# Low parts of four heads and of all mixing inputs computed by the vector engine in PSUM, and stage entries re-ordered, in a hybrid two-block model on one core

## The chip, the cores and the metric

The kernel runs on one core of one Trainium2 chip. The metric is the device time of one execution in microseconds (us). Five engines work side by side: TensorE (PE, matrix products into PSUM), VectorE (DVE), ScalarE (ACT), GpSimd (POOL) and SyncE (SP, which issues the weight loads). They order their work by semaphores alone.

## What is computed

The reference chains two blocks over 16 meta tokens and 256 tokens of width 1024. Block one mixes two branches (a gated recurrence of 8 heads, "hg", and a latent attention, "mla"), projects the mixture, and ends with a feed-forward part. Block two runs two layers of a convolution beside a sparse attention. Cut to what the change touches:

```python
# block one
o = rms_norm(o, norm_g) * silu(g)                       # hg heads
y_a, y_b = o @ w_hg_o, mla @ w_mla_o
mixed = (gate_a * y_a + gate_b * y_b) @ w_out           # "mix"
h = h + rms_norm(mixed, mix_post_g)
gt, up = split(rms_norm(h, ffn_pre_g) @ w_ffn_in)
h = h + rms_norm((silu(gt) * up) @ w_ffn_out, ffn_post_g)
# block two, twice
y = concat([silu(layer_norm(conv)) * silu(zc), attention * silu(za)]) @ w_out_2[l]
h = layer_norm(ALPHA * h + y, post_ln_g, post_ln_b)
```

## The kernel before

Activations lie transposed: 128 features on the partitions, tokens along the free axis (256, or 272 with the meta tokens), so a width of 1024 is 8 tiles c = 0 to 7. Each weight product is made from three fast products: every operand x is rounded to a high part (x_hi) and a low part x_lo = x - x_hi, and `three` (L603) issues w_hi·x_hi, w_hi·x_lo and w_lo·x_hi. One `chunk` (128 output features) is 8 steps of three matmuls, 24 in all. `chunks_together` (L629) interleaves two or three chunks step by step, so that the first steps need only the first tiles of x; the last two steps (`tail`) run side by side at the end.

**Weights.** SP loads items of 256 columns into a ring of 3 slots. Each item is two pieces. ACT rounds a piece into w_hi (`round_piece`, L1264) after the chunk that frees one of the 4 buffers; POOL subtracts it into w_lo (`lo_piece`, L1139), and that frees the slot. POOL's program is one fixed list, in which the x subtractions (`lo_x`, L1153) stand between the weight subtractions.

**Entry of a stage.** PE can begin a stage when the first x_hi and x_lo are there, w_lo is there, and the PSUM bank (`bank_free`, L581) has been read. Where it would wait, the program puts in dummy products (`turns_over`, L686). The entries concerned are:

- **hgo**, eight chunks of the output product of the hg heads, in turns on PSUM banks 0 and 1. Its input y_hg is made by DVE (L1930), rounded by ACT (L1469), subtracted by POOL (L1196). DVE then multiplies each chunk in its bank by gate_a (L1944) and adds the gated mla part into `ya` in SBUF (L1945); that add frees the bank. Ahead of these, `gate_mla` (L1918) multiplies the eight mla chunks by gate_b, all operands in SBUF.
- **mix**, the projection. Its input is `ya`, rounded by ACT (L1474, each behind a weight piece) and subtracted by POOL (L1202).
- **ffi**, entered through `add_normed` (L1948: scale, then add to hT), **L0h**, the entry of block two through the same helper, **L1h** behind the first layer's normalisation (ACT writes hT and x_hi, L1691 and L1692).
- **wo**, the output product of a layer. Its eight inputs are four conv tiles (ACT Silu L1644, DVE product L2167) and four attention tiles (DVE L2173 out of PSUM), all rounded by ACT (L1610) and subtracted by POOL (L1238). The last chunk before it is za 3, whose 8 steps `z_chunks` (L208) spreads over the last attention steps; ACT reads it out at L1654 behind the Silu of three gates (L1649), and that frees the bank. x_hi is still read by za 3, so no new x_hi may be written before its end. PE turns the attention output by transposes (L1072) just ahead of wo.

Of the kernel before, what the change touches and what calls it, by code (L numbers as in the profile page):

```python
# [176 lines left out]
for _c in range(DC):  # L177
    PLN_DVE += [f"b{_c}"] + ([f"a{_c + 2}"] if _c + 2 < DC else [])
# [28 lines left out]

def z_chunks(l, s):  # L208
# [72 lines left out]
OUT, _outs = [], dict(chunk_out=0, gated=0, h_mid=0, h_ready=0, state=0)  # L281
GATED = ["L0a0", "L0a1", "L1a0", "L1a1"] + [f"hgo{_j}" for _j in range(4)] + [f"ffi{2 * _j + 1}" for _j in range(FFN_ITEMS)]
for _n, _m in ORDER:
    _by = "gated" if _n in GATED else "h_mid" if _n.startswith("mix") else "h_ready" if _n == "ffo" \
        else "state" if _n == "S" else "chunk_out"
# [9 lines left out]
def bass_blocks(nc, a, out):  # L295
    ctx = ExitStack()
    with ctx:
# [95 lines left out]
        ya, f_sq = z(DC, SEQ), z(DC, SEQ)  # L393
# [184 lines left out]
        def _(pe):  # L578
# [302 lines left out]
            chunks_together([part("hgo", c) for c in range(2)], (y_hi, y_lo), 0, x_ready("hg"))  # L881
            for c in range(2, DC):
                chunk(*part("hgo", c), (y_hi, y_lo))
            turns_over(3, 3)
            linear_norm("post", [lambda: chunks_together([part("mix", c) for c in range(2)], X, META, x_ready("mix"))]
# [17 lines left out]
            turns_over(3, BANK[CHUNK[part("ffi", 1)]])  # L903
# [33 lines left out]
            for l in range(DEPTH2):  # L937
# [5 lines left out]
                turns_over((12, 10)[l], BANK[CHUNK[part(f"{T}g", 1)]])  # L943
                chunks_together([part(f"{T}g", 0), part(f"{T}g", 1), part(f"{T}a", 0)], X, 0, x_ready(f"{T}h"))
# [191 lines left out]
        def _(pool):  # L1136
# [56 lines left out]
            for h in range(HEADS):  # L1193
                if h < 6 and h % 2 == 0:
                    lo_piece(SPLIT["hgo0", 0] + h // 2)
                lo_x("hg", h, y_lo[:, h, :], y_hg[:, h, :], y_hi[:, h, :])  # L1196
            lo_piece(SPLIT["hgo1", 1])
            lo_items("hgo2", "hgo3")
            for c in range(DC):
                if c in (5, 6):  # L1200
                    lo_piece(SPLIT["mix0", c - 5])
                lo_x("mix", c, x_lo[:, c, META:L], ya[:, c, :], x_hi[:, c, META:L])  # L1202
            lo_items("mix1", "ffi1")
# [16 lines left out]
            for l in range(DEPTH2):  # L1220
                T = f"L{l}"
                q_from = 0 if l == 0 else META
                for c in range(DC):
                    lo_x(f"{T}h", c, x_lo[:, c, :], hT[:, c, :], x_hi[:, c, :])
# [12 lines left out]
                for c in range(DC):  # L1237
                    lo_x(f"{T}y", c, x_lo[:, c, q_from:L], ycat[:, c, q_from:L], x_hi[:, c, q_from:L])  # L1238
# [5 lines left out]
        def _(act):  # L1244
# [222 lines left out]
            for c in range(4, DC):  # L1467
                for h in (2 * c - 8, 2 * c - 7):
                    split("hg", h, y_hi[:, h, :], y_hg[:, h, :], (sem("y_hg"), h + 1))  # L1469
# [45 lines left out]
            for l in range(DEPTH2):  # L1515
# [90 lines left out]
                def split_y(c):  # L1606

                    if c == 0:
                        act.wait_ge(sem("chunk_done"), CHUNK[f"{T}za1", 1] + 1)
                    split(f"{T}y", c, x_hi[:, c, q_from:L], ycat[:, c, q_from:L], (sem("y"), DC * l + c + 1))  # L1610

# [21 lines left out]
                for s in range(DSA_N[l] + DSA_LAG + 1):  # L1633
# [6 lines left out]
                    if s == DSA_N[l] + DSA_LAG:  # L1640
                        for c in range(CC + 1):
                            if c < CC:
                                act.wait_ge(sem(f"{T}cln_scaled"), c + 1)
                                af(ycat[:, c, q_from:L], acc[:, c, q_from:L], ACT.Silu, scale=vec("conv_ln_g_2", 4 * l + c),  # L1644
                                   bias=vec("conv_ln_b_2", 4 * l + c)).then_inc(sem("c_silu"), 1)
# [671 lines left out]
```

## Time and profile before

| | us |
|---|---|
| three runs | 922.62, 922.79 (median), 922.9 |
| the profiled execution | 922.45 |
| its span in the profile | 920.6 |
| PE busy | 881.6 (96%) |
| POOL busy | 617.8 (67%) |
| DVE busy | 501.7 (54%) |
| ACT busy | 474.6 (52%) |

The span is the stretch covered by the trace; 1.85 us of the execution lie around it. Busy PE is not PE at its peak, since matmuls overlap: each row of 0.28 us begins 0.118 us (0.124 us with 272 columns) after the last. What a change can win is seen in the idle time of PE ahead of a stage.

### The profile page before, as it was taken

To read this page: it belongs to the slowest core of one execution; us is meant where nothing else is said; L and a number is where in the kernel's file an instruction comes from. 1 tells how busy PE (TensorE), PEld (TensorE's weight loads), DVE (VectorE), ACT (ScalarE), POOL (GpSimd) and SP (SyncE) were. 2 spreads that over 40 slices of the span, in tenths; PEclk is the share of its full clock that TensorE was granted. 3 is DMA by queue.
4 is the path that set the end of the run, shared out by engine and by line. 5 is a ranking of instruction groups with operands and counts; after the bars stand their busy time and mean duration, and the time that the engine had idled before them with its cause. 6 is when DMAs were issued, how large, how long until landed. Compare 5 with 4: busy or idle time off the path is not lost.

```text
span 920.6 us, 17060 instructions
## 1 busy us (share of the span) xinstructions
PE 881.6 (96%) x6817; PEld 841.0 (91%) x6817; DVE 501.7 (54%) x1090; ACT 474.6 (52%) x930; POOL 617.8 (67%) x360
## 2 busy tenths in 40 slices
PE   5999999999999999999999999999998999999986
PEld 4995999999999898999999998999987989999776
DVE  3304111599828637655331115878954658799545
ACT  5425755633356446544444444445657554456672
POOL 4712655655556997999998897776854777766142
PEclk9999999999999999999999999999999999999998
DMA  8522743443432455455655672654220627544201
GB/s 269 173 80 92 231 135 97 133 138 93 138 102 96 158 195 183 133 189 185 199 157 169 190 209 83 204 172 138 101 93 1 183 60 213 157 138 160 70 1 46
DMA packets 134478, 128.09 MB, mean 139 GB/s; under 512 B 6496, under 2 KB 132064, under 8 KB 134400
## 3 DMA queue, kind: packets, MB, share of 16 engines
q1 hardware_dynamic: 133920, 126.20, 44.3%
q8 instruction: 55, 0.90, 0.4%
q10 hardware_dynamic: 480, 0.79, 0.2%
q14 instruction: 23, 0.19, 0.1%
HBM read 125.80 MB, written 1.05 MB: 138 GB/s over the span
## 4 chain that ended last, share of the span: by engine, by line
PE 83%; DVE 7%; POOL 4%; ACT 4%; DMA 1%; issue 1%; DVEq 0%; ACTq 0%
PE PS L605 22%; PE PS L607 22%; PE PS L606 22%; PE PS L832 3%; POOL w_lo L1146 3%; PE PS L596 2%; PE PS L972 1%; PE PS L742 1%; DVE PS L2019 1%; PE PS L794 1%; PE PS L1032 1%; DMA ring<-in_w_in 1%; ACT w_hi L1269 1%; POOL y_lo L1156 1%; PE PS L790 1%
## 5 line engine op out<-in xcount | busy, mean ns | idle before, releaser
L1146 POOL TENSOR_TENSOR w_lo<-ring,w_hi 128x1024 fp32r<-128x1024 f32 (+1 forms) x235 | 539.5, 2310 | 253.8 <-ACT w_hi L1269 243.3
L605 PE MATMUL PS<-x_hi,w_hi 128*128 128x256 f32 (+2 forms) x1560 | 459.5, 295 | 10.9 <-ACT zoneB L1252 4.8
L607 PE MATMUL PS<-x_hi,w_lo 128*128 128x256 f32 (+2 forms) x1560 | 444.9, 285 | 0.0
L606 PE MATMUL PS<-x_lo,w_hi 128*128 128x256 f32 (+2 forms) x1560 | 443.9, 285 | 0.0
L605 PEld LDWEIGHTS PS<-x_hi,w_hi 128*128 128x128 f32 (+1 forms) x1560 | 294.9, 189 | 16.0 <-issue 13.1
L606 PEld LDWEIGHTS PS<-x_lo,w_hi 128*128 128x128 f32 (+1 forms) x1560 | 294.4, 189 | 1.4 <-issue 0.2
L607 PEld LDWEIGHTS PS<-x_hi,w_lo 128*128 128x128 f32 (+1 forms) x1560 | 294.5, 189 | 0.0
L1269 ACT ACTIVATE w_hi<-ring 128x1024 fp32r<-128x1024 f32 (+2 forms) x233 | 235.5, 1014 | 80.7 <-PE PS L607 77.4
L2019 DVE SCALAR_TENSOR_TENSOR PS<-zoneA,cols,PS 128x256 f32<-128x256 f32 x240 | 98.7, 482 | 0.1
L1252 ACT ACTIVATE zoneA<-PS 128x272 f32<-128x272 f32 (+3 forms) x76 | 29.3, 386 | 108.7 <-PE PS L607 108.7
L1252 ACT ACTIVATE zoneB<-PS 128x256 f32<-128x256 f32 (+4 forms) x115 | 40.9, 378 | 75.9 <-DVE PS L1986 38.3
L1986 DVE TENSOR_TENSOR PS<-PS,nrm 128x256 f32<-128x256 f32 x44 | 18.7, 430 | 61.8 <-PE PS L607 61.7
L605 PE MATMUL PS<-hid_hi,w_hi 128*128 128x256 f32 x176 | 49.1, 279 | 0.0
L607 PE MATMUL PS<-hid_hi,w_lo 128*128 128x256 f32 x176 | 49.1, 279 | 0.0
L606 PE MATMUL PS<-hid_lo,w_hi 128*128 128x256 f32 x176 | 49.1, 279 | 0.0
L1752 DVE TENSOR_TENSOR nrm<-nrm,sq 128x256 f32<-128x256 f32 x10 | 14.3, 1427 | 37.0 <-ACT sq L1286 37.0
L1814 DVE CUSTOM_DVE_ANT_0 zoneB<-PS,const 128x144 f32<-128x144 f32 (+1 forms) x16 | 6.0, 375 | 51.3 <-PE PS L791 51.3
L605 PEld LDWEIGHTS PS<-hid_hi,w_hi 128*128 128x128 f32 x176 | 33.1, 188 | 0.0
L606 PEld LDWEIGHTS PS<-hid_lo,w_hi 128*128 128x128 f32 x176 | 33.1, 188 | 0.0
L607 PEld LDWEIGHTS PS<-hid_hi,w_lo 128*128 128x128 f32 x176 | 33.1, 188 | 0.0
L1744 DVE RECIPROCAL nrm<-nrm 128x256 f32<-128x256 f32 (+1 forms) x7 | 12.6, 1794 | 35.6 <-ACT nrm L1294 35.6
L832 PE MATMUL PS<-zoneA 128*128 128x128 f32 x256 | 31.1, 275 | 0.0
(290 smaller groups left out, 1205.1 us busy)
## 6 DMA issues: line engine op xcount, KB each, us to landing
ring<-in_w_in SPq DMA_DIRECT2D x58, 1024.0 KB, 5.5
ring<-in_w_ffn_in SPq DMA_DIRECT2D x22, 1024.0 KB, 5.1
ring<-in_w_out SPq DMA_DIRECT2D x12, 1024.0 KB, 5.0
ring<-in_w_ffn_out SPq DMA_DIRECT2D x16, 704.0 KB, 4.5
ring<-in_w_mla_o SPq DMA_DIRECT2D x4, 1024.0 KB, 5.0
ring<-in_w_hg_o SPq DMA_DIRECT2D x4, 1024.0 KB, 5.0
ring<-in_w_kv_b SPq DMA_DIRECT2D x2, 1024.0 KB, 5.3
ring<-in_w_q_b SPq DMA_DIRECT2D x2, 768.0 KB, 4.8
```

The lines of the kernel that those rows point to most:

```text
L596: last = mm(PS[0:rows, BANK[g], 0:n], lhs(i), rhs(i), start=(i == 0), stop=(i == k - 1))
L605: mm(out_, hi_w, hi_x, start=start, stop=False)
L606: mm(out_, hi_w, lo_x, start=False, stop=False)
L607: return mm(out_, lo_w, hi_x, start=False, stop=stop)
L832: last = mm(PS[:, 2 + 2 * half + b, j * P:(j + 1) * P], hk[:, h, tok], hq[:, h, tok], start=True, stop=True)
L1146: sub(lo_w, src, hi_w, ALU.subtract).then_inc(sem("w_lo"), 1)
L1252: ins = af(dst, view(src) if view else src, f, **kw)
L1269: af(hi_w, src, ACT.Copy).then_inc(sem("w_hi"), 1)
L1744: link(v.reciprocal(buf, buf))
L1752: v.tensor_tensor(total, total if c > 1 else square(0), square(c), ALU.add).then_inc(sem(f"sum_{tag}"), 1)
L1986: return y, v.tensor_tensor(y, y, nrm[:, 1, 0:SEQ], ALU.mult)
L2019: ins = v.scalar_tensor_tensor(out=total, in0=upad[:, c, META + j:j + L], scalar=w, in1=total, op0=ALU.mult, op1=ALU.add)
```

## The change

1. **hgo's input.** The y of heads 4 to 7 stays in PSUM. DVE, not POOL, makes the low parts of these four (`low_hg`), between its gate products.
2. **mix's input.** The mixture stays in its PSUM bank. ACT rounds it from there, and DVE, not POOL, makes the low part of all eight; this last operation, not the add, now frees the bank. ACT rounds two weight pieces (after hgo 0 and hgo 1) ahead of the first mixture tile. POOL's list loses 12 x subtractions; three turns ahead of mix go.
3. **ffi and L0h.** `add_normed` does the first add ahead of the second scaling. The copy of the meta rows moves ahead of the reciprocal. Turns: 3 to 5 ahead of ffi, 12 to 10 ahead of L0h.
4. **L1h.** ACT writes x_hi ahead of hT; the first low part is made by DVE.
5. **wo, both layers.** DVE rounds the four conv tiles itself, in the order y0 y1 hi0 hi1 y2 y3 hi2 hi3; ACT reads za 3 out ahead of the Silu of the three gates; the steps of za 3 are spread 1, 2, 2, 3 (layer 0; before 1, 1, 2, 4) and 1, 1, 2, 2, 2 (layer 1; before 1, 1, 1, 1, 4).

```diff
-    for s_, steps in ((n - 2, 1), (n - 1, 1), (n, 1), (n + 1, 1), (n + 2, 4)) if l else ((n - 1, 1), (n, 1), (n + 1, 2), (n + 2, 4)):
+    for s_, steps in ((n - 2, 1), (n - 1, 1), (n, 2), (n + 1, 2), (n + 2, 2)) if l else ((n - 1, 1), (n, 2), (n + 1, 2), (n + 2, 3)):
...
-            turns_over(3, 3)
...
-                turns_over((12, 10)[l], BANK[CHUNK[part(f"{T}g", 1)]])
+                turns_over(10, BANK[CHUNK[part(f"{T}g", 1)]])
...
             for c in range(DC):
-                round_after(*part("hgo", c))
-                split("mix", c, x_hi[:, c, META:L], ya[:, c, :], (sem("gated"), OUT[CHUNK[part("hgo", c)]][1]))
+                for i in ((0, 1) if c == 0 else (c,) if c > 1 else ()):
+                    round_after(*part("hgo", i))
+                split("mix", c, x_hi[:, c, META:L], PS[:, BANK[CHUNK[part("hgo", c)]], 0:SEQ],
+                      (sem("y_first"), HEADS + c + 1))
...
-                        for c in range(CC + 1):
-                            if c < CC:
...
-                            if c:
-                                split_y(c - 1)
-                        out_of_psum(act, *part(f"{T}za", 2))
-                        af(sza[:, 0:3, q_from:L], sza[:, 0:3, q_from:L], ACT.Silu).then_inc(sem("z_gates"), 1)
+                        for c in range(CC):
...
                         take(*part(f"{T}{n}", m), (szc if n == "zc" else sza)[:, m, q_from:L],
                              ACT.Silu if last else ACT.Copy, n=n_q, ahead=not last)
+                        if last:
+                            out_of_psum(act, *part(f"{T}za", 2))
+                            af(sza[:, 0:3, q_from:L], sza[:, 0:3, q_from:L], ACT.Silu).then_inc(sem("z_gates"), 1)
...
+            def low_hg(pair):
+
+                for h in (2 * pair, 2 * pair + 1):
+                    dve.wait_ge(sem("hi_hg"), 2 * pair + 2)
+                    v.tensor_tensor(y_lo[:, h, :], PS[:, 2 + pair, h % 2 * SEQ:h % 2 * SEQ + SEQ], y_hi[:, h, :],
+                                    ALU.subtract).then_inc(sem("lo_by_dve"), 1)
...
+                if pair == 3:
+                    low_hg(2)
                 gate_mla(pair)
+            low_hg(3)
...
                 link(v.tensor_tensor(y, y, gates[:, c, :], ALU.mult))
-                v.tensor_tensor(ya[:, c, :], y, y_mla[:, c, :], ALU.add).then_inc(sem("gated"), 1)
+                v.tensor_tensor(y, y, y_mla[:, c, :], ALU.add).then_inc(sem("y_first"), 1)
+                dve.wait_ge(sem("hi_mix"), c + 1)
+                v.tensor_tensor(x_lo[:, c, META:L], y, x_hi[:, c, META:L], ALU.subtract).then_inc(sem("lo_by_dve"), 1)
...
+                product(0)
+                added(0, 0)
+                product(1)
+                for c in range(1, DC):
+                    if c + 1 < DC:
+                        product(c + 1)
+                    added(c, c + 1 < DC)
...
             add_squares("fpost")
+            link(v.tensor_copy(hT[:, :, 0:META], meta_rows[:, :].rearrange("p (c t) -> p c t", c=DC)))
             rstd("fpost", 1, nrm[:, 0, 0:SEQ])
-            link(v.tensor_copy(hT[:, :, 0:META], meta_rows[:, :].rearrange("p (c t) -> p c t", c=DC)))
...
+                    else:
+                        dve.wait_ge(sem("chunk_done"), CHUNK[f"{T}za1", 1] + 1)
+                        dve.wait_ge(sem("y"), y_at(l, f"y{c}"))
+                        v.tensor_copy(x_hi[:, c, q_from:L], ycat[:, c, q_from:L]).then_inc(sem("y"), 1)
...
+                    if c == 1:
+                        dve.wait_ge(sem(f"hi_L{l + 1}h"), 1)
+                        step("l0", v.scalar_tensor_tensor(out=x_lo[:, 0, :], in0=zT[:, 0, :],
+                                                          scalar=vec("post_ln_b_2", 8 * l), in1=x_hi[:, 0, :],
+                                                          op0=ALU.add, op1=ALU.subtract))
```

## Rows read from the trace of the kernel before

**Rows 1.** The page, part 1: busy us, share of the span, instructions.

```profile
PE 881.6 (96%) x6817; PEld 841.0 (91%) x6817; DVE 501.7 (54%) x1090; ACT 474.6 (52%) x930; POOL 617.8 (67%) x360
```

**Rows 2.** Timeline of PE at the entries: start, us, line, idle before and releaser.

```profile
305.97 0.36 PE L605 MATMUL PS<-y_hi,w_hi 128*128 128x256 f32 x1 [0.68 <-ACT zoneA L1252]
...
313.65 0.35 PE L605 MATMUL PS<-y_hi,w_hi 128*128 128x256 f32 x1 [0.48 <-DVE zoneA L1945]
...
330.54 1.46 PE L689 MATMUL PS<-const 128*128 128x256 f32 x6
332.71 0.35 PE L605 MATMUL PS<-x_hi,w_hi 128*128 128x256 f32 x1 [0.72 <-POOL w_lo L1146]
...
361.63 0.36 PE L605 MATMUL PS<-x_hi,w_hi 128*128 128x256 f32 x1 [1.67 <-DVE x_lo L1973]
...
557.57 0.36 PE L605 MATMUL PS<-x_hi,w_hi 128*128 128x272 f32 x1 [1.37 <-POOL x_lo L1156]
...
707.96 0.36 PE L605 MATMUL PS<-x_hi,w_hi 128*128 128x272 f32 x1 [1.75 <-ACT zoneB L1252]
...
740.42 0.36 PE L605 MATMUL PS<-x_hi,w_hi 128*128 128x272 f32 x1 [1.40 <-DVE zoneB L2238]
...
884.84 0.36 PE L605 MATMUL PS<-x_hi,w_hi 128*128 128x256 f32 x1 [3.08 <-ACT zoneB L1252]
```

**Rows 3.** One line's instructions: ns min/median/max over all of them.

```profile
L1920 DVE TENSOR_TENSOR zoneA<-zoneA,zoneB x8: 419/952/2625, 285.2 to 308.9; 128x256 f32<-128x256 f32 x8
...
L1945 DVE TENSOR_TENSOR zoneA<-PS,zoneA x8: 424/425/426, 313.1 to 331.2; 128x256 f32<-128x256 f32 x8
...
L1756 DVE CAST hid_hi<-zoneB x22: 293/1060/2459, 375.9 to 489.2; 128x256 fp32r<-128x256 f32 x22
```

**Rows 4.** Timelines of DVE, POOL and ACT around hgo, 302 to 314 us.

```profile
302.11 7.71 DVE L1920 TENSOR_TENSOR zoneA<-zoneA,zoneB 128x256 f32<-128x256 f32 x5
...
312.62 0.43 DVE L1944 TENSOR_TENSOR PS<-PS,zoneB 128x256 f32<-128x256 f32 x1 [2.79 <-PE PS L607]
313.08 0.42 DVE L1945 TENSOR_TENSOR zoneA<-PS,zoneA 128x256 f32<-128x256 f32 x1
...
306.10 2.58 POOL L1146 TENSOR_TENSOR w_lo<-ring,w_hi 128x1024 fp32r<-128x1024 f32 x1
...
312.52 1.06 ACT L1269 ACTIVATE w_hi<-ring 128x1024 fp32r<-128x1024 f32 x1 [5.85 <-PE PS L607]
313.54 0.42 ACT L1279 ACTIVATE x_hi<-zoneA 128x256 fp32r<-128x256 f32 x1
```

**Rows 5.** Timelines at the entry of L0h: POOL, then DVE.

```profile
545.42 9.38 POOL L1146 TENSOR_TENSOR w_lo<-ring,w_hi 128x1024 fp32r<-128x1024 f32 x4 [0.50 <-ACT w_hi L1269]
556.66 5.88 POOL L1156 TENSOR_TENSOR x_lo<-hT,x_hi 128x272 fp32r<-128x272 f32 x8 [1.86 <-ACT x_hi L1279]
...
553.39 1.49 DVE L2000 COPY hT<-meta_rows 128x128 f32<-128x128 f32 x1
```

**Rows 6.** Timelines ahead of wo and L1h, layer 0: PE's transposes, ACT.

```profile
703.78 0.29 PE L1069 MATMUL PS<-zoneB 16*64 16x16 f32 x4
...
705.77 0.44 PE L1072 MATMUL PS<-const,zoneB 128*128 128x128 f32 x2
...
700.67 1.10 ACT L1644 ACTIVATE zoneB<-zoneA,cols 128x272 f32<-128x272 f32 x2
...
738.50 0.52 ACT L1691 ACTIVATE hT<-zoneB,cols 128x272 f32<-128x272 f32 x1 [2.46 <-DVE zoneB L2243]
```

**Rows 7.** Windows view, 699 to 703 us: five busy times, then the granted clock.

```profile
699.00:703.00 4.00, 3.92 (x20) 3.92 (x21) 1.64 (x5) 2.40 (x5) 0.00 (x0) 0.57 0.01 4
```

**Rows 8.** Timelines ahead of wo, layer 1: ACT, PE's transposes, POOL.

```profile
879.29 1.08 ACT L1644 ACTIVATE zoneB<-zoneA,cols 128x256 f32<-128x256 f32 x2
...
880.72 1.03 PE L1072 MATMUL PS<-const,zoneB 128*128 128x128 f32 x8
...
881.42 0.64 POOL L1156 TENSOR_TENSOR x_lo<-zoneB,x_hi 128x256 fp32r<-128x256 f32 x1 [8.85 <-ACT x_hi L1279]
```

More of the change, by code:

```diff
@@ L205, with y_at @@
 TAPS_AT_ATT = {3: 115, 4: 118, 5: 121, 6: 124}
+Y_ORDER = ["y0", "y1", "hi0", "hi1", "y2", "y3", "hi2", "hi3"] + [f"y{_c}" for _c in range(CC, DC)]
+def y_at(l, name):
+    return len(Y_ORDER) * l + Y_ORDER.index(name) + 1
 def z_chunks(l, s):
@@ L279 @@
 BEFORE = [max([_p for _p in range(_g) if BANK[_p] == BANK[_g]], default=None) for _g in range(len(ORDER))]
-OUT, _outs = [], dict(chunk_out=0, gated=0, h_mid=0, h_ready=0, state=0)
-GATED = ["L0a0", "L0a1", "L1a0", "L1a1"] + [f"hgo{_j}" for _j in range(4)] + [f"ffi{2 * _j + 1}" for _j in range(FFN_ITEMS)]
+OUT, _outs = [], dict(chunk_out=0, gated=0, h_mid=0, h_ready=0, state=0, lo_by_dve=4)
+GATED = ["L0a0", "L0a1", "L1a0", "L1a1"] + [f"ffi{2 * _j + 1}" for _j in range(FFN_ITEMS)]
 for _n, _m in ORDER:
     _by = "gated" if _n in GATED else "h_mid" if _n.startswith("mix") else "h_ready" if _n == "ffo" \
-        else "state" if _n == "S" else "chunk_out"
+        else "state" if _n == "S" else "lo_by_dve" if _n.startswith("hgo") else "chunk_out"
     if _n[2:-1] == "wo":
@@ L878, in _ @@
                 chunk(*part("mlo", c), X, META)
-            chunks_together([part("hgo", c) for c in range(2)], (y_hi, y_lo), 0, x_ready("hg"))
+            chunks_together([part("hgo", c) for c in range(2)], (y_hi, y_lo), 0,
+                            lambda i: pe.wait_ge(sem("lo_hg" if i < 4 else "lo_by_dve"), i % 4 + 1))
             for c in range(2, DC):
                 chunk(*part("hgo", c), (y_hi, y_lo))
-            turns_over(3, 3)
-            linear_norm("post", [lambda: chunks_together([part("mix", c) for c in range(2)], X, META, x_ready("mix"))]
+            linear_norm("post", [lambda: chunks_together([part("mix", c) for c in range(2)], X, META,
+                                                          lambda i: pe.wait_ge(sem("lo_by_dve"), 4 + i + 1))]
                         + [lambda c=c: chunk(*part("mix", c), X, META, free=(sem("sq_post"), c - 3) if c >= 4 else None)
@@ L902, in _ @@
             bank_free(CHUNK[part("ffi", 1)])
-            turns_over(3, BANK[CHUNK[part("ffi", 1)]])
+            turns_over(5, BANK[CHUNK[part("ffi", 1)]])
             chunks_together([part("ffi", c) for c in range(3)], X, META,
@@ L1192, in _ @@
             lo_items("mlo2", "mlo3")
-            for h in range(HEADS):
-                if h < 6 and h % 2 == 0:
-                    lo_piece(SPLIT["hgo0", 0] + h // 2)
+            for h in range(4):
+                if h % 2 == 0:
+                    lo_piece(SPLIT["hgo0", h // 2])
                 lo_x("hg", h, y_lo[:, h, :], y_hg[:, h, :], y_hi[:, h, :])
[L1197 to L1203, printed above, removed]
+            lo_items("hgo1", "ffi1")
             for c in range(DC):
```

88 lines of the change are left out of this document (50 added, 38 removed).

## Prediction

> **What bounds the kernel now.** The page comes first [rows 1]: PE is busy for 881.6 of 920.6 us, and no other engine is above 67%. So nothing that another engine saves counts in itself; a change can only win or lose in PE's 39 us of idle time, or in the dummy turns that fill some of it. Second, the timeline of PE at the entries of the stages [rows 2]: its brackets give the idle time and what ended it. The reader is to see six entries with 0.7 to 3.1 us each, and that each is ended by another engine's small operation (a subtraction, a bank being read out), not by a weight load. Third, for each entry, the timelines of the engines that release it [rows 4 to 6, 8]. Fourth, one line's shortest and longest times [rows 3], since DVE's cost hangs on its neighbour.
>
> **What DVE pays beside POOL.** A DVE product whose two inputs lie in SBUF takes 0.42 us at best and 2.63 at worst, the rounding copy from SBUF to SBUF 0.29 to 2.46, while the product with one input in PSUM takes 0.424 to 0.426 in all eight cases, beside a POOL that never rests [rows 3]. So DVE's work in PSUM is priced flat at 0.42, and its work in SBUF as: wait for the end of POOL's running instruction, then run. Five gate products in a row take 7.71 us, one to each POOL instruction [rows 4]. The Trainium skill ("SBUF — State Buffer", section "SBUF: two separate sides") has the rule: the port pair that DVE and GpSimd share is an exclusive lock, held for a whole instruction by an operation with two SBUF inputs or in a two-port mode, and the other blocks fully. The trace agrees, and the rule speaks against part 5 of the change, which puts roundings from SBUF to SBUF beside POOL's subtractions; if it didn't hold there, wo of layer 1 would gain 2.8 us rather than the 1.7 below.
>
> **hgo and mix.** PE enters hgo at 305.97, released by ACT's reading of a bank [rows 2]; that is not touched. Then it paused for POOL's low parts of heads 4 to 7 (about 1.1 us in all until 313.65), since POOL makes them behind the 2.58 us subtraction begun at 306.10 [rows 4]. Now DVE makes them in PSUM: two pairs of 0.42, the first at about 302.1, the second behind ACT's rounding of heads 6 and 7, both done near 305.4, ahead of PE. So 48 matmuls of 0.118 run through, and the two chunks end at 311.1 and 311.8.
>
> Here the change adds a wait. Hgo 2 needs the bank of hgo 0, which was free after gate and add (0.46 and 0.42 from 312.62, PE on at 313.65) [rows 2, 4]. Now it is free only after ACT's rounding and DVE's subtraction, and ACT first rounds two weight pieces. ACT: 311.15, plus 1.02 and 0.95 for two pieces, gives 313.1, plus 0.4 for the tile (start to start 1.02) [rows 4]. DVE: the gate products lose short POOL instructions to hide between and take one slot of 2.4 us each, so the eighth ends near 312.1 instead of 309.8; gate and add end at 313.1, about when ACT is ready. Rounding to 313.5, subtraction 0.42 and 0.15 for semaphores: PE goes on at 314.2, 0.55 later than before, having stood for 2.3 us. Queued behind DVE's new wait are only gate and add of hgo 1, whose low part ends near 315.9, and hgo 3 wants it at 317.1. From then on a bank is held for 1.95 us (ACT 1.05 and 0.4, DVE 0.42, semaphores) against the 2.83 us of a chunk: covered, with 0.9 to spare. If that cover went, each of six chunks would pay.
>
> Six chunks took 330.54 - 313.65 = 16.9 us. They end at 331.1, and mix follows at once: its first low parts are long there, POOL has 12 subtractions of some 0.74 less ahead of w_lo, and the last low part (near 333) is asked for 4.2 us after the start. Before, turns and a wait for w_lo filled 330.54 to 332.71. Gain 332.71 - 331.1 = **1.6 us**. Bounds: 1.1 if a gate product meets one more POOL instruction, 2.1 if none does.
>
> **ffi.** The low part of tile 0 released PE at 361.63 [rows 2]. As many DVE operations (two scalings more, two adds) stand ahead of it as before; only the first add now follows its own scaling, 0.46 start to start (312.62 to 313.08) instead of 0.40 [rows 4]. Two more turns (0.24 a pass, 1.46 for six, so about 1 us) [rows 2] fit into the 1.67 idle. **-0.1 us.**
>
> **L0h.** The copy of the meta rows costs 1.49 on the path, waiting for POOL until 554.8 [rows 5]. Ahead of the reciprocal it lies in idle time of DVE. First add 0.35 earlier as well, so x_hi is ready at 554.8. What is late next is POOL, which ends its weights at 545.42 + 9.38 = 554.80 [rows 5], then needs 0.75 for the first low part: PE at 555.7. The turns ended at 556.2; ten instead of twelve (four passes less) end at 555.3. Gain 557.57 - 555.7 = **1.85**, bounds 1.4 and 2.0. The eight low parts come every 0.74 (5.88 for eight) against 1.1 for a step of three chunks, so nothing else stalls.
>
> **wo, layer 0.** The bank of za 3 was read last in ACT's queue and released PE at 707.96; the transposes had ended at 706.2 [rows 2, 6]. Now ACT does four Silu at 0.50 from 700.67, then reads the bank, by 703.9; DVE rounds tile 0 at the end of za 3, POOL's first low part comes 1.2 us after it. What is late next is PE itself: one step (three matmuls, 0.37) moves from behind the last attention product into a gap ahead of it, so za 3 ends at 703.45 rather than 703.84, and 2.4 us of transposes (703.78 to 706.2) [rows 6] end at 705.9. The low parts of tiles 1 to 7, every 0.7, stay ahead of PE's 0.75 per step. Gain **2.0**. It stands on the clock: the granted clock is 0.57 over 699 to 703 [rows 7], that is at 1.2 GHz for 3.4 of the 4 us, after a PE with idle gaps of 0.8 us, and matmuls there begin 0.23 apart instead of 0.124. I take the dip as unchanged.
>
> **L1h.** x_hi takes the place of hT at 738.50 [rows 6]; 0.5 later DVE makes the first low part (0.48), PE starts at 739.75 instead of 740.42. But the second low part stays POOL's, behind the same four ACT operations as before (some 0.41 each from 738.50), so I keep it at 741.15; a step is 1.1. Gain **0.35** (0.1 to 0.7).
>
> **wo, layer 1.** Idle 3.08 ahead of 884.84; transposes done at 881.75 [rows 2, 8]. Now: Silu from 879.29 at 0.50, bank read by 881.7; DVE y0, y1, then hi0 at 881.05; POOL's first low part takes 0.64 [rows 8]; PE starts at 881.9. Then the shared port bites: y2, hi2 and hi3 and POOL's subtractions take turns, so the low parts come at 881.8, 882.75, 884.0, 884.95, 885.75, then every 0.65, where PE would take one each 0.71. PE ends the two chunks near 889.0; before, 884.84 plus 48 x 0.118 gives 890.6. Gain **1.7**; bounds 1.1 (each DVE operation waits a whole subtraction more) and 2.8 (no waits).
>
> **Sum.** 1.6 - 0.1 + 1.85 + 2.0 + 0.35 + 1.7 = 7.4 us. Span 920.6 - 7.4 = 913.2. The profiled execution, 922.45, would be 915.05; it lies 0.34 below the median of the runs, 922.79, from which I take 7.4: **915.4**. With the bounds of the terms, added as independent, 914.0 to 916.9.
>
> **The rivals.**
> - *The clock stays up in layer 0* (0.24). The extra step fills part of the gap ahead of the dip. For: layer 1 has gaps as long and no dip. Then o products and nine matmuls save 1.4 us, of which ACT and the low parts leave 1.3: **914.1**.
> - *The entries do not open as said* (0.14): POOL or the lock is what PE then waits for, so that each rounding on DVE costs a whole subtraction and PE's pauses are moved behind the first steps; mix keeps only half. Then L0h (1.85) and half of the other 5.55 are left, less 0.7: **918.8**.
> - *The bank hold becomes the bound of hgo* (0.04), the side slower than before. Mechanism: DVE's add and new subtraction have one input in SBUF and could wait for POOL as the gate products do. It decides from a hold over 2.83 us. If both waited half a POOL instruction of 2.4, the hold is 4.35, 1.5 too much in six chunks, 9.1, and 2.4 at the first: **926.9**. Against: 0.425 in eight of eight cases [rows 3].
> - *A new dip* (0.05): PE stands 2.3 us at 312 and falls to 1.2 GHz for 3.4 us; that costs 1.7: 917.1. Against: it kept its clock over 3.08 us in layer 1.
>
> **How the numbers follow.** The forecast has 0.53. About 0.2% (1.85 us) is what a measurement of this kernel can tell from no change. The range goes from below the clock rival to the case of closed entries: 912.9 to 918.8. Faster needs under 920.9: forecast, clock, dip and nearly all of the closed entries, 0.92; slower 0.04; same 0.04.
>
> **What would show it.** PE enters mix straight behind hgo without a gap, after a pause of some 2.3 us at 312 ended by DVE's subtraction (1.6 right); L0h begins 1.85 us earlier in relation to the reciprocal, released by POOL; wo of layer 0 follows the transposes; in layer 1 PE starts near 3 us sooner and then has short pauses ended by POOL. DVE's new subtractions at 0.42 refute the slow rival. It would be wrong if the pause at 312 is well over 2.3 us, if a pause appears between hgo 3 and 7, or if an entry is released by a line not named here.

## The result and the profile after

The changed kernel takes 912.61 us (median of four runs, 911.52 to 914.27) where the kernel before, run beside it, takes 922.85: the ratio is 0.9876, with a 95% interval of 0.9858 to 0.9894. On a second chip, with more runs of both, it was 0.9867 (0.9845 to 0.9889). The forecast was 915.4, with a range down to 912.9; the gain is 10.2 us instead of 7.4 and lies just outside.

The page of the changed kernel, part 1 (busy us, share of the span, instructions); its span is 909.6 us in a run of 911.52. It answers to [rows 1].

```profile
PE 877.5 (96%) x6811; PEld 837.6 (92%) x6811; DVE 510.0 (56%) x1111; ACT 471.7 (52%) x922; POOL 609.2 (67%) x347
```

PE's idle time went from 39.0 to 32.1 us, and its busy time fell by 4.1. The second number is already a hint: apart from some dummy turns the matmuls are the same ones, so a part of them ran at a higher clock.

The timeline of PE at the entries, changed kernel (start us, us, line, idle before and releaser), beside [rows 2]:

```profile
304.84 0.36 PE L614 MATMUL PS<-y_hi,w_hi 128*128 128x256 f32 x1 [0.68 <-POOL y_lo L1168]
...
312.90 0.36 PE L614 MATMUL PS<-y_hi,w_hi 128*128 128x256 f32 x1 [2.22 <-DVE x_lo L1970]
...
329.78 0.28 PE L614 MATMUL PS<-x_hi,w_hi 128*128 128x256 f32 x1
...
358.78 0.35 PE L614 MATMUL PS<-x_hi,w_hi 128*128 128x256 f32 x1 [0.95 <-DVE x_lo L2009]
...
552.68 0.36 PE L614 MATMUL PS<-x_hi,w_hi 128*128 128x272 f32 x1 [0.52 <-POOL x_lo L1168]
...
699.00 0.44 PE L1084 MATMUL PS<-const,zoneB 128*128 128x128 f32 x2
699.19 0.37 PE L614 MATMUL PS<-x_hi,w_hi 128*128 128x272 f32 x1
...
731.01 0.36 PE L614 MATMUL PS<-x_hi,w_hi 128*128 128x272 f32 x1 [0.76 <-DVE x_lo L2300]
...
873.18 0.36 PE L614 MATMUL PS<-x_hi,w_hi 128*128 128x256 f32 x1 [0.59 <-POOL x_lo L1252]
```

The pause of hgo is one pause of 2.22 us now, ended by VectorE's subtraction. Mix (329.78) has no bracket because it follows hgo without a gap: it begins 24.94 us behind hgo's entry (26.74 before). Hgo's own entry, which the change was not to touch, now has GpSimd's `y_lo` in its bracket where it had ScalarE's reading of a bank; the wait is 0.68 us as before, and the distance to it from the 254 us mark explained below is 51.50 and 51.60 us (51.63 and 51.64 before), so nothing was lost there. The wait of 1.75 us ahead of layer 0's output product is gone: the product (699.19) follows the last transpose (699.00) directly.

Distances between these entries, in us. A stage that is entered late doesn't charge the next one, so each line can be read alone. "Before again" and "changed again" are second profiles of the two unchanged files.

| from, to | before | before again | changed | changed again |
|---|---|---|---|---|
| start, hgo | 305.97 | 305.88 | 304.84 | 305.90 |
| hgo, ffi | 55.66 | 55.61 | 53.94 | 53.92 |
| ffi, L0h | 195.94 | 195.94 | 193.90 | 193.87 |
| L0h, wo of layer 0 | 150.39 | 150.39 | 146.51 | 146.54 |
| wo of layer 0, L1h | 32.46 | 32.47 | 31.82 | 31.83 |
| L1h, wo of layer 1 | 144.42 | 144.42 | 142.17 | 142.15 |
| wo of layer 1, end | 35.76 | 38.39 | 36.42 | 36.39 |
| span | 920.6 | 923.1 | 909.6 | 910.6 |

Two lines stand out. The first line differs by 1.0 us between the two profiles of one and the same changed file, and the last by 2.6 us between the two of the kernel before.

The granted clock where [rows 7] showed the fall, windows view (five busy times, then the granted clock), changed kernel:

```profile
699.00:703.00 4.00, 4.00 (x36) 4.00 (x33) 2.42 (x7) 2.57 (x6) 3.41 (x6) 1.00 0.00 0
```

The clock is 1.00 there, 2.4 GHz throughout.

The new work of VectorE, one line's instructions in the changed kernel (ns min/median/max): the eight low parts of the mixing input, and the four of hgo's heads 4 to 7.

```profile
L1970 DVE TENSOR_TENSOR x_lo<-PS,x_hi x8: 425/425/425, 312.3 to 331.3; 128x256 fp32r<-128x256 f32 x8
...
L1940 DVE TENSOR_TENSOR y_lo<-PS,y_hi x4: 407/412/414, 301.0 to 303.8; 128x256 fp32r<-128x256 f32 x4
```

Twelve of twelve take 0.41 to 0.425 us beside a busy GpSimd: the flat price read off [rows 3] holds for the new operations, with one input in PSUM.

### The profile page after: what moved, and what is told of

It is laid out like the page before. It is cut to its first block, busy times and chain, and to the rows that moved or that the text cites. A ratio compares the mean times of both kernels' runs of the same rounds, so it can differ in the third digit from the quotient of the medians.

```text
span 909.6 us, 17053 instructions
## 1 busy us (share of the span) xinstructions
PE 877.5 (96%) x6811; PEld 837.6 (92%) x6811; DVE 510.0 (56%) x1111; ACT 471.7 (52%) x922; POOL 609.2 (67%) x347
## 4 chain that ended last, share of the span: by engine, by line
PE 87%; DVE 6%; ACT 3%; issue 1%; DMA 1%; POOL 1%; DVEq 0%; ACTq 0%
PE PS L614 23%; PE PS L616 23%; PE PS L615 23%; PE PS L841 3%; PE PS L605 2%; PE PS L751 1%; PE PS L984 1%; DVE PS L2055 1%; PE PS L803 1%; ACT w_hi L1284 1%; PE PS L1044 1%; DMA ring<-in_w_in 1%; PE PS L799 1%; PE PS L800 1%; PE PS L1015 1%
```

## The experiments

The questions were: did the clock stay up because of the change, and by which part of it; what is each part worth; and is the rest of the difference real. The "start" mark used below is the first transpose of the value stage, at 254 us; nothing ahead of it was changed in any of the kernels. Chips and hours differ, and the kernel before had 920 to 928 us in the runs beside these experiments, so small differences are read from the profiles' distances and not from medians.

### The clock in layer 0: the spread of the gate tile

The old spread in the changed kernel:

```
-    ... (n, 2), (n + 1, 2), (n + 2, 2)) if l else ((n - 1, 1), (n, 2), (n + 1, 2), (n + 2, 3)):
+    ... (n, 1), (n + 1, 1), (n + 2, 4)) if l else ((n - 1, 1), (n, 1), (n + 1, 2), (n + 2, 4)):
```

> The changed kernel with the last eight steps of layer 0's fourth gate tile (and of layer 1's) spread over the attention as before: one step between the last two waits of TensorE instead of two. Theory A: the longer stretch of idle TensorE at 698 to 699 us of the kernel before is what made the granted clock fall to 0.50 for 3.4 us there, and the second step in that place is what keeps it up now. Then the fall is back in this kernel, and the time is 1.7 (3.4 us at half the speed) + 0.4 (the two waits are filled less, 1.06 instead of 0.69 between two starts) = 2.1 us longer than the changed kernel, 914.3 to 915.2. Rival B: the fall went with something upstream, or comes and goes by itself: the clock stays at 1.00 here and the time is 0.4 us longer than the changed kernel, about 913.0.

Measured: 915.22 us, against 912.0 and 912.6 for the changed kernel. First the timeline of PE ahead of the last wait, then the windows view (five busy times, granted clock) of the stretch behind it:

```profile
695.48 0.28 PE L1035 MATMUL PS<-const,zoneB 128*16 128x128 f32 x1 [0.78 <-DVE zoneB L2188]
```

```profile
696.30:699.70 3.40, 3.40 (x18) 3.40 (x18) 1.56 (x3) 2.78 (x5) 0.00 (x0) 0.54 0.00 0
```

The idle time is 0.78 us again, and right behind it the clock is at 0.54, half speed for nearly the whole stretch. L0h to wo takes 148.44 us instead of 146.51: 1.9 longer, as theory A said. But the fall is no certainty: one of its four runs had a mean clock of 0.996 and took 912.2. Two others had 0.990 and took 915.8 and 916.4, more than one fall of 3.4 us explains; the edit puts back layer 1's old spread as well, and no profile shows what fell in those two.

The new spread alone in the kernel before (the reverse of the same two lines):

> The kernel before with nothing but the new spread of the fourth gate tile's steps in both layers. Theory A (the spread alone keeps the clock up): no fall at 699 us, and a gain of 1.7 + 0.4 = 2.1 us at the first transpose into the turned banks, of which the old order of ScalarE ahead of the output product keeps some back, since that chain (Silu, Silu, four Copies, bank read) does not start earlier: 1.0 to 2.1 us faster than before, 920.8 to 921.9. Rival B (the fall has another cause): it stays, and the time is 0 to 0.4 us under that of before.

Measured: 924.54 us, ratio 1.0005 (0.9989 to 1.0021), no gain. The profile says why, in the timeline of PE and in the windows view:

```profile
699.34 0.28 PE L1023 MATMUL PS<-const,zoneB 128*16 128x128 f32 x1 [0.41 <-DVE zoneB L2152]
...
706.29 0.57 PE L605 MATMUL PS<-x_hi,w_hi 128*128 128x272 f32 x1 [1.75 <-ACT zoneB L1252]
```

```profile
705.90:709.30 3.40, 3.01 (x13) 3.04 (x14) 1.48 (x4) 2.76 (x7) 2.13 (x4) 0.51 0.00 0
883.40:890.20 6.80, 5.94 (x28) 5.97 (x29) 1.42 (x4) 4.39 (x9) 5.07 (x6) 0.50 0.00 0
```

The fall at 699 us is gone as theory A said, L0h to wo is 148.56 (1.83 less), and then the clock falls at 705.9 instead, in the 1.75 us wait ahead of the output product, and once more in layer 1. The fall was postponed, not removed. Neither A nor B had this.

Idle matmuls instead of moved work, first in one pause of the kernel before:

```
+                    if l == 0 and s == DSA_N[0]:
+                        turns_over(3, 7)
```

> The kernel before with three idle matmuls of 256 columns (some 0.33 us, into a bank that nothing reads then) put behind the fourth gate tile's step in front of the last wait of layer 0's attention (L1023, idle 0.78 us). Nothing else differs, no work is moved. Theory A (idle time of TensorE just there makes the clock fall): no fall at 699 us, the first transpose 1.4 to 1.7 us earlier, and 1.0 to 1.7 us less in all if the wait for ScalarE ahead of the output product lets it through, otherwise 0. Rival B: the fall stays and the time is that of before within 0.3 us.

I had sized the dummies wrongly: one takes 0.43 us, not 0.11, so three filled the pause and pushed the transpose behind it by 0.4 us (it begins 141.93 us behind the entry of L0h, before 141.51). Measured: 923.93 us, ratio 0.9998 (0.9983 to 1.0013). The profile has no fall in layer 0 (L0h to wo 149.26, 1.1 less), and one of 6.8 us in layer 1, at 882.2.

Then with the right size, in three pauses:

```
+                    if l == 0 and s == DSA_N[0]:
+                        turns_over(1, 7)
...
+                turns_over((3, 6)[l], 4)
                 chunks_together([part(f"{T}wo", c) for c in range(2)], X, q_from, x_ready(f"{T}y"))
```

> The kernel before, no work moved, with idle matmuls (0.43 us each) in three pauses of TensorE: one ahead of the last wait of layer 0's attention (0.78 us of idle time), three ahead of layer 0's output product (1.75 us), six ahead of layer 1's (3.08 us). Theory A (idle TensorE at these places is what lets the granted clock fall, at 699 us in one run, at 706 or 883 us in another): the runs keep the clock at 0.995 or more where most of the kernel before have 0.989 to 0.992, and the median is 2 to 3 us under that of before, about 921.5; the entries' own waits end where they did. Rival B (the falls come from elsewhere or by themselves): the clocks are spread from 0.984 to 0.997 as before, and the time is that of before within 0.5 us.

Measured: 922.41 us against 925.02, ratio 0.9967 (0.9954 to 0.9981). So 2.6 us come from the clock alone: no work was taken away or moved, only idle time filled. The clocks of its eight runs are 0.993 (five), 0.994 and 0.990 (two), where nine of 13 runs of the kernel before beside them have 0.989 or 0.990. In layer 0 the profile shows no fall, and L0h to wo takes 148.90, so the fall costs 150.39 - 148.90 = 1.5 us. In layer 1 a fall stayed, which costs 1.7 us (L1h to wo 146.13 instead of 144.42), but it begins ahead of the filled wait (timeline of PE, windows view):

```profile
870.82 0.88 PE L1032 MATMUL PS<-zoneB 128*128 128x64 f32 x6 [0.99 <-ACT zoneB L1627]
...
872.75 0.55 PE L1021 MATMUL PS<-const,zoneB 128*128 128x128 f32 x3 [0.63 <-ACT zoneB L1633]
```

```profile
873.60:880.40 6.80, 6.80 (x34) 6.80 (x34) 1.95 (x7) 4.78 (x9) 0.00 (x0) 0.51 0.00 0
```

Ahead of it PE stood 0.99 and 0.63 us within 2 us, two pauses well under the 3.08 us that I had filled.

### The order of ScalarE and VectorE ahead of the output products

The changed kernel with the new spread and the old order (ScalarE makes all high parts and reads the bank behind them):

```
-                        for c in range(CC):
+                        for c in range(CC + 1):
...
+                            if c:
+                                split(f"{T}y", c - 1, x_hi[:, c - 1, q_from:L], ycat[:, c - 1, q_from:L], (sem("y"), DC * l + c))
+                        out_of_psum(act, *part(f"{T}za", 2))
...
-                for name in Y_ORDER[:2 * CC]:
+                for c in range(CC):
```

> The changed kernel, its new spread kept, with ScalarE's and VectorE's order ahead of the two output products as before: ScalarE makes the high parts of the first four tiles between its Silus and reads the gate tile's bank behind them. Forecast: 1.6 us at layer 0's product (2.0 less the 0.4 that the spread gives) and 1.7 us at layer 1's, 3.3 us in all, so 915.9 where the changed kernel had 912.6; the waits there read 1.7 and 3.1 us again. Rival (the clock): with those two pauses back the granted clock falls there in most runs too, 0.992 or less, and the time is another 2 to 3 us longer, 918 to 919.

Measured: 919.63 us, ratio to the kernel before 0.9946 (0.9926 to 0.9966), so 7 us longer than the changed kernel. All six of its runs have a clock of 0.987 to 0.993. The timeline of PE and the windows view:

```profile
701.68 0.56 PE L614 MATMUL PS<-x_hi,w_hi 128*128 128x272 f32 x1 [1.75 <-ACT zoneB L1262]
...
879.33 0.55 PE L614 MATMUL PS<-x_hi,w_hi 128*128 128x256 f32 x1 [3.19 <-ACT zoneB L1262]
```

```profile
700.90:704.30 3.40, 2.62 (x11) 2.65 (x12) 1.48 (x4) 2.42 (x7) 1.60 (x4) 0.58 0.01 2
878.40:881.80 3.40, 2.47 (x11) 2.50 (x12) 1.42 (x4) 2.79 (x7) 2.01 (x4) 0.58 0.00 0
```

Both hold: the two waits are back, 2.0 us in layer 0 (L0h to wo 148.52 against 146.51) and 2.2 in layer 1 (144.39 against 142.17), of which the end gives back 0.66; and the clock falls in each of them. The forecast's 3.3 us were 3.6 by these distances. Two falls of 3.4 us at 1.4 us each (wo of layer 0 to L1h takes 33.26 us instead of 31.83, and the end 37.2 instead of the 35.8 of the old order) are most of the rest. The 2.2 us of layer 1 contain a loss of 0.37 us that the changed kernel has within the attention and this one has not; the experiment on layer 1's entry below comes back to it.

### The entries of hgo, mix, L0h and L1h

The changed kernel with hgo's and mix's entries as before (all low parts on GpSimd, three turns ahead of mix):

```
-                            lambda i: pe.wait_ge(sem("lo_hg" if i < 4 else "lo_by_dve"), i % 4 + 1))
...
+            turns_over(3, 3)
...
-                if pair == 3:
-                    low_hg(2)
                 gate_mla(pair)
-            low_hg(3)
...
-                v.tensor_tensor(x_lo[:, c, META:L], y, x_hi[:, c, META:L], ALU.subtract).then_inc(sem("lo_by_dve"), 1)
```

> The changed kernel with the entries of hgo and of the mixing product as before: all eight low parts of hgo's input and all of mix's on GpSimd, the outputs of the gated products in SBUF, three idle matmuls ahead of mix. Theory (the forecast's step): these two entries are worth 1.6 us, and the profile gave 1.9; the time is 1.6 to 1.9 us longer than that of the changed kernel, 914.2 to 914.5. Rival: some of the 1.9 belongs to chance in the first stages, and this part is worth under 1.2 us; or later stages give back some of it and the time is 0.5 to 1.0 longer only.

Measured: 914.59 us, 2.0 to 2.6 longer than the changed kernel's medians. Hgo to ffi takes 55.79 us against 53.92: 1.9; from the mark to the end it is 658.07 us against 656.29 and 656.34. The theory stands, at its upper end. The 55.79 are also 0.13 more than the kernel before has there (55.66): the price of ffi's new order, forecast at 0.1.

The copy of the meta rows back behind the reciprocal:

```
-            link(v.tensor_copy(hT[:, :, 0:META], meta_rows[:, :].rearrange("p (c t) -> p c t", c=DC)))
             rstd("fpost", 1, nrm[:, 0, 0:SEQ])
+            link(v.tensor_copy(hT[:, :, 0:META], meta_rows[:, :].rearrange("p (c t) -> p c t", c=DC)))
```

> The changed kernel with the copy of the 16 rows that all inputs share back behind the reciprocal, ahead of layer 0's first product. The forecast put 1.5 of that entry's 1.85 us down to this copy; the profile gave 2.04 for the entry. So the wait of TensorE there reads 1.9 to 2.1 instead of 0.52 us, the entry starts 1.4 to 1.5 us later, and the time is 1.5 us longer than that of the changed kernel, 914.1. Rival: the copy overlaps what ScalarE and GpSimd do behind the first sum, and its move is worth under 0.7 us; the new order of the sums (the first one ahead of the second product) brought the rest.

Measured: 913.27 us, and at the entry of L0h

```profile
554.76 0.36 PE L614 MATMUL PS<-x_hi,w_hi 128*128 128x272 f32 x1 [2.00 <-POOL x_lo L1168]
```

2.00 us of idle time instead of 0.52; from the 254 us mark to L0h it is 300.81 us against 299.34 and 299.39, so 1.4 to 1.5 longer. The copy's place is worth what was said.

Layer 1's entry as before:

```
-                    af(x_hi[:, c, :], zT[:, c, :], ACT.Identity, **affine).then_inc(sem(f"hi_L{l + 1}h"), 1)
                     af(hT[:, c, q_from:L], zT[:, c, q_from:L], ACT.Identity, **affine).then_inc(sem("h_post"), 1)
+                    af(x_hi[:, c, :], zT[:, c, :], ACT.Identity, **affine).then_inc(sem(f"hi_L{l + 1}h"), 1)
...
-                        step("l0", ...)
```

> The changed kernel with layer 1's entry as before: ScalarE writes the normed tile ahead of its high part, and GpSimd makes the first low part from the finished tile. Forecast 0.35 us net (0.64 at the entry in the profile, given back by 0.19 at the second step): the wait at the entry reads 1.4 instead of 0.76 us and everything behind it is 0.4 to 0.5 us later. The time is 0.4 us longer, which the runs can hardly tell; the profile's distance from the output product's start to the entry of layer 1 tells it, 32.46 us instead of 31.82. Rival: the new order also moved the later first products of layer 1, and 1 us or more is lost here.

Measured: 913.43 us (911.48 to 914.54), which can't be told from the changed kernel. The wait at the entry reads 1.40 us and wo to L1h takes 32.46, as expected. But from the 254 us mark to wo of layer 1 it is 874.44 - 254.53 = 619.91 us, and in the changed kernel's second profile 874.21 - 254.30 = 619.91 as well. So in this comparison nothing of the 0.64 us is left. The first 0.29 go at the next product of layer 1 (9.86 us behind the entry instead of 9.57), the second low part being late as forecast. That leaves 0.35, the forecast. The other 0.37 go within the attention, where one product with the values begins 0.59 us behind its transposes (854.35 behind 853.76) instead of 0.33 (854.67 behind 854.34). This loss is in both profiles of the changed kernel, in that of the old spread and in those of the two tries at the end. It is not in three others that have the same new entry: from L1h to wo of layer 1 the kernel with hgo and mix as before and the one with the copy back take 141.80 us, 0.37 less than 142.17, and the one with the old order has the product at 0.33 too. So the entry alone doesn't bring it, and what does is not shown.

### What the runs give by themselves

The kernel before and the changed kernel once more, nothing edited.

> The kernel before, unchanged, for one more profile of it. Three of the profiles so far have the 254 us mark (the first transpose of the value stage) at 254.3 to 254.6, one at 254.0, and that of the changed kernel at 253.34, though nothing ahead of it was changed. If that mark varies from run to run, it lies between 253.3 and 254.7 here; and the clock falls at 699, 706 or 883 us or at two of them, not at the same place as in the first profile of necessity. If it is a property of the kernel, it is 254.3 within 0.1.

Measured: 924.91 us, the mark at 254.24, and two falls:

```profile
699.70:703.10 3.40, 3.40 (x18) 3.40 (x18) 1.57 (x3) 1.84 (x3) 0.00 (x0) 0.55 0.03 5
884.00:890.80 6.80, 6.09 (x30) 6.12 (x31) 1.42 (x4) 4.24 (x9) 4.92 (x6) 0.52 0.00 0
```

The second, 6.8 us at half speed, lies where the first profile had none, and explains the 2.6 us of the last line of the table (38.39 instead of 35.76).

> The changed kernel, unchanged, beside more runs of the kernel before on one chip. Theory A (two thirds of what the forecast missed is the clock: the kernel before loses 1.5 us at each fall, the changed kernel seldom has one): the changed kernel's runs have clocks of 0.994 to 0.996 and 911.5 to 914.3 us, most of before's 0.989 to 0.992 and 923 to 925 us, so the ratio is 0.986 to 0.988, lower than the 0.9876 of the first chip or equal to it; the mark at 254 us is not 253.34 again but nearer to 254.2. Rival B: the changed kernel has falls as often on this chip; the ratio is 0.989 to 0.991, that of the terms without the clock.

Measured: six runs of 911.65 to 912.45 us, all at a clock of 0.996; the kernel before beside them 920.1 to 928.3, with clocks of 0.984 to 0.997; ratio 0.9867 (0.9845 to 0.9889). The mark is at 254.30. Theory A stands. Over all 14 profiles the mark lies between 253.34 and 254.64, in both kinds of kernels: the 1.0 us that the changed kernel's first profile had ahead of hgo was chance, not a gain.

The 43 runs of the kernel before beside the experiments sort themselves by their mean granted clock:

| clock | runs | span, us |
|---|---|---|
| 0.997 | 2 | 918.3 to 919.0 |
| 0.995 | 7 | 920.6 to 921.3 |
| 0.991, 0.992 | 6 | 921.0 to 922.1 |
| 0.989, 0.990 | 25 | 922.7 to 924.3 |
| 0.984 | 3 | 926.0 to 926.4 |

The profiles say what stands behind three of the lines (none was taken of a run with 0.997 or 0.984): the first profile of the kernel before (0.995) has the short fall alone, the one with idle matmuls in one pause (0.992) the long one alone, the second profile of the kernel before (0.990) both. Of the changed kernel's ten runs nine have 0.996 and one 0.994; both its profiles show no fall but that at the very end, which all kernels have. Without falls the kernel before takes 918 to 919 us of span (its two runs at 0.997; 920.6 less the 1.5 of the short fall is 919.1), the changed one about 910.

### Two tries for a faster kernel

```
-                for i in ((0, 1) if c == 0 else (c,) if c > 1 else ()):
+                for i in (c,):
```

> The changed kernel with one weight piece rounded by ScalarE ahead of each mixing input instead of two ahead of the first. In the changed kernel's profile ScalarE rounds two pieces (2.00 us from 310.02) before the first high part (311.93), while VectorE has had the sum since 311.4, and TensorE pauses 2.22 us at the third gated product. Theory: the second piece holds the high part back by 0.5 us (to when VectorE's sum is there), the pause reads 1.75 us and the kernel is 0.4 to 0.5 us faster. Rival: the second piece is what the mixing product wants early, it comes 1 us later in its order, TensorE waits for it in the products behind, and the gain is given back: same time within 0.2 us, or slower.

Measured: 912.6 us. The pause is shorter by what was said:

```profile
312.81 0.36 PE L614 MATMUL PS<-y_hi,w_hi 128*128 128x256 f32 x1 [1.79 <-DVE x_lo L1970]
```

From the 254 us mark to the end the profile has 655.7 us, against 656.3 in both profiles of the changed kernel. The gain of 0.4 to 0.6 us is there and isn't given back, but the median doesn't show it: three of its six runs have a clock of 0.996 (911.1 to 912.0 us), the others 0.991 to 0.994 (913.2 to 914.0).

```
-Y_ORDER = ["y0", "y1", "hi0", "hi1", "y2", "y3", "hi2", "hi3"] + ...
+Y_ORDER = ["y0", "hi0", "y1", "hi1", "y2", "y3", "hi2", "hi3"] + ...
...
+                    if l == 0 and i == DSA_TILES + 1:
+                        turns_over(1, 7)
...
-                for i in ((0, 1) if c == 0 else (c,) if c > 1 else ()):
+                for i in (c,):
```

> Three edits at once on the changed kernel, as a try for a faster one: the piece order of the run before this one (0.45 us if the theory holds), the first high part ahead of the second product at both output products (0.2 us at layer 1's entry, whose wait of 0.59 us ends with GpSimd's first low part; 0 at layer 0's, which has no wait), and one idle matmul in layer 0's last pause but one (0.76 us), against the clock. If all hold: 0.6 us faster than the changed kernel and clocks never under 0.994. Rival: VectorE's high part straight behind its own product waits for that product's write and shifts the second product, so that nothing is gained at layer 1; then it equals the run with the pieces alone.

Measured: 912.42 us. L1h to wo is 142.14 us, so the earlier first high part brought nothing, and the dummy didn't keep the clock up in all runs (three at 0.996, three at 0.993 and 0.994). No version tried is measurably faster than the changed kernel.

## Why the forecast was low

By the steps of the sum; the gain is measured between kernels without a fall of the clock where there are such profiles.

- **hgo, mix and ffi: 1.5 forecast, 1.7 measured** (55.66 to 53.94). The mechanism is the one described: no pauses for heads 4 to 7, one pause of 2.22 us (2.3 forecast) ended by VectorE's subtraction, no gap ahead of mix, ffi later by 0.1. PE goes on 8.06 us behind the entry of hgo where the forecast had 8.2 (314.2); 0.13 of the difference is a slip in the forecast's own addition, since 313.5 + 0.42 + 0.15 is 314.07. The gate products were priced too high, without harm: the last one ends 5.67 us behind the entry, not 6.1, so VectorE was ready ahead of ScalarE and not together with it. ScalarE's second piece held the first rounding, which the first try for a faster kernel shows. The gates, then ScalarE's rounding of two pieces and of the tile, and VectorE's subtraction, changed kernel's timelines:

```profile
304.12 6.39 DVE L1933 TENSOR_TENSOR zoneA<-zoneA,zoneB 128x256 f32<-128x256 f32 x4
...
311.01 0.43 DVE L1968 TENSOR_TENSOR PS<-PS,zoneA 128x256 f32<-128x256 f32 x1
312.32 0.42 DVE L1970 TENSOR_TENSOR x_lo<-PS,x_hi 128x256 fp32r<-128x256 f32 x1 [0.88 <-ACT x_hi L1294]
...
310.02 2.00 ACT L1284 ACTIVATE w_hi<-ring 128x1024 fp32r<-128x1024 f32 x2 [4.49 <-PE PS L616]
311.93 0.36 ACT L1294 ACTIVATE x_hi<-PS 128x256 fp32r<-128x256 f32 x1
```

- **L0h: 1.85 forecast, 2.05 measured** (195.94 to 193.90). POOL was next, as said: its first low part begins 0.12 us behind its weights. The weights themselves end 0.3 us earlier than I had assumed from [rows 5]: 192.87 us behind the entry of ffi instead of 193.17.

```profile
542.24 9.41 POOL L1158 TENSOR_TENSOR w_lo<-ring,w_hi 128x1024 fp32r<-128x1024 f32 x4 [0.50 <-ACT w_hi L1284]
551.77 0.76 POOL L1168 TENSOR_TENSOR x_lo<-hT,x_hi 128x272 fp32r<-128x272 f32 x1
```

- **wo of layer 0: 2.0 forecast, 3.9 measured, and this is the step that failed.** 1.5 of it are the clock: "I take the dip as unchanged" was wrong. The rival "the clock stays up in layer 0" had 1.3 us for it, and I gave it 0.24. Its mechanism was half of what the runs showed: it put the clock down to the extra step in the gap, but with that step alone the fall came 6.6 us later, in the wait ahead of the output product. The new order, which removes this wait, was needed as well. The other 0.4 are in the sum itself: without the fall the stage goes from 148.90 to 146.51, 2.4 us. The order of ScalarE and VectorE is worth 2.0 of this by its own experiment, and the spread 0.34 (148.90 to 148.56). Some 0.25 of the missing 0.4 are an estimate from the timelines and no run separates them: I had taken the end of the last transpose (706.2) as the moment from which the product can start, but in the changed kernel the product starts at 699.19 while the row of the last two transposes lasts until 699.44.
- **L1h: 0.35 forecast, 0.35 measured up to the second step.** The entry opens 0.64 us earlier, and the late second low part takes 0.29 back. By wo of layer 1 the other 0.35 are gone too, in the loss within the attention whose cause is open; the forecast had no such term.
- **wo of layer 1: 1.7 forecast, 2.2 measured.** From L1h to wo 144.42 to 142.17, plus the 0.64 us that are given back on the way there, is 2.9 us for the entry, as forecast (884.84 to 881.9); the pauses behind it take 0.66 (35.76 to 36.42), where 2.9 less 1.7 had left 1.2 for them. So the step that was mis-sized is the turn-taking of VectorE and GpSimd: the low parts of tiles 2, 3 and 4 are there 1.8, 2.4 and 3.0 us behind the entry and not 2.1, 3.05 and 3.85. Only y2 and y3 were slowed; hi2 and hi3 began while GpSimd was idle and took 0.28 us each. The spread is part of the 2.9: it brings 0.29 with the old order (144.13 with the spread alone) and 0.14 with the new one (142.31 with the old spread). The kind of pause is the one foreseen: VectorE's y2 and y3 take 0.83 us each, where y0 and y1 take 0.37, and PE waits for POOL again at the second step.

```profile
871.36 0.75 DVE L2205 TENSOR_TENSOR zoneB<-zoneB 128x256 f32<-128x256 f32 x2
872.02 0.49 DVE L2210 CAST x_hi<-zoneB 128x256 fp32r<-128x256 f32 x2
872.43 1.67 DVE L2205 TENSOR_TENSOR zoneB<-zoneB 128x256 f32<-128x256 f32 x2
...
872.39 1.42 POOL L1252 TENSOR_TENSOR x_lo<-zoneB,x_hi 128x256 fp32r<-128x256 f32 x2 [8.57 <-DVE x_hi L2210]
...
875.07 0.39 PE L614 MATMUL PS<-x_hi,w_hi 128*128 128x256 f32 x1 [0.22 <-POOL x_lo L1252]
```

- **The sum.** Without falls: 1.7 + 2.05 + 2.4 + 0.35 - 0.35 + 2.2 = 8.35, so 8.4 us where 7.4 were forecast. One fall of 1.5 us gives 9.9, and the measured difference of the first medians is 10.2. The profiled pair has 11.0, with 1.0 of chance ahead of hgo. So of the 2.8 us that I missed, 1.5 are the clock; four terms were 0.2 to 0.5 short each, 1.3 together, less the 0.35 lost in layer 1's attention; the 0.3 left are within the scatter of the runs.
- **The other rivals.** Entries that don't open: not one. The bank hold: the subtraction takes 0.425 in eight of eight cases, and no pause follows at the later gated products. A new fall at 312: none in any profile, in spite of a pause of 2.22 us. But my reason against it, that layer 1 kept its clock over 3.08 us [rows 2], was read from one execution: 34 of the 43 later runs have a mean clock under that of this profile, and all four later profiles of kernels built on it (unchanged, spread alone, two with idle matmuls) show the long fall in layer 1.
- **The range.** Its lower end, 912.9, was the clock rival with 1.2 us to spare. The terms' own excess and the clock came together, both on the same side, and the range hadn't room for both.

What stays open is by what rule the clock falls. In the profiles it falls behind or in idle time of PE around the ends of the two attentions, and filling or removing that time makes it rarer or moves it; but one of four runs with the old spread had none, and the changed kernel keeps its clock with pauses of 0.99 and 0.64 us at 864 us that are as long as those ahead of a fall in the kernel with idle matmuls. That the pair of changes (spread and order) keeps the falls away is shown by the profiles: seven were taken of kernels that have both changes, and none of these shows a fall ahead of the one at the end; seven were taken of kernels that lack one or both, and each of these shows one or two. By the clocks of the runs it makes them rarer and doesn't exclude them. With the order undone six of six runs fall, with the spread undone three of four, with both and nothing else edited one of ten; but of the 24 runs of the five other kernels that have both, ten have a clock of 0.994 or less. Four runs are few for the spread.

## What to carry to other kernels

Where a profile shows the clock below 1.00 in a stretch, price a change that fills or removes idle time just ahead of it twice, with and without the fall, and ask for the next pause behind it: closing the first alone only moved the fall 6.6 us on and gained nothing that the runs can tell (ratio 1.0005). Read the mean granted clock of every run beside its time before explaining a difference of less than 1%; here it sorts the runs of one unchanged kernel from 918 to 926 us. And price a removed wait from start to start and not from the modelled end of a matmul: in this kernel that end lay 0.25 us behind the start of the next one.

## What the runs showed of the hardware

- One kernel on one core takes 918.3 to 926.4 us of span, sorted by its mean granted clock. In the profiles a fall to 0.5 (1.2 GHz) lasts 3.4 us and costs 1.4 to 1.5 us, or 6.8 us and costs 1.7 to 2.7; part of it lies in or ahead of a wait of TensorE. The first three runs, 922.62 to 922.9, hid this. The Trainium skill ("TensorE: Matmul & The Clock Gate", section "Part 1: The HAM clock gate (the "warmup" mystery)") says that the number of slow matmuls at the start of a kernel differs between runs of the same kernel. It speaks of the start alone; here it is the falls in the middle of the kernel that differ between runs, as the table above shows.
- Falls came behind pauses of 0.6 to 1.0 us (0.76 and 0.78 at 697 and 699 us; 0.99 and 0.63 at 871 and 873 us) and within waits of 1.75 to 3.2 us ahead of an output product (the windows at 701, 706, 879 and 884 us above), while one pause of 2.22 us between dense matmuls, at 312 us, brought none in any of the eight profiles that have it or its 1.8 us form.
- VectorE's operations with one input in PSUM take 0.41 to 0.425 us beside a running GpSimd in all twelve new cases, and its products with two inputs in SBUF 0.83 (y2 and y3 beside GpSimd's subtractions) instead of 0.37 (y0 and y1 ahead of them).
